# Two more 1 MB places for the experts' weights, and another order in which the chunks use the places

## The reference

```python
def hier_moe(h, router_group_w, router_expert_w, w_gate, w_up, w_down):
    ...   # each token is sent to TOP_K = 2 experts of one group
    def expert_block(args):
        xblk, e = args
        a = xblk @ w_gate[e]          # 1024 x 512
        b = xblk @ w_up[e]            # 1024 x 512
        return (jax.nn.silu(a) * b) @ w_down[e]    # 512 x 1024
    ...   # weighted by the gate and added to the tokens
```

## Time and profile before

| | |
|---|---|
| median of three runs | 1726.66 us (1725.32 to 1726.68) |
| the profiled execution | 1725.77 us |
| its span in the profile | 1724.0 us |
| TensorE busy | 1622.8 us, 94% |
| VectorE busy | 988.2 us, 57% |
| ScalarE busy | 611.1 us, 35% |
| moved by DMA | 415.65 MB, 241 GB/s over the span |

### The profile page before, as it was taken

The page is one execution under the profiler, slowest core; times in us unless marked ns, Lnnn a source line. Parts: engine busy times, 40 slices in busy tenths (PEclk is TensorE's granted clock), DMA queues, the critical chain, the costliest instruction groups (busy, mean ns, idle before and its releaser), DMA issues.

```text
span 1724.0 us, 25871 instructions
## 1 busy us (share of the span) xinstructions
PE 1622.8 (94%) x10376; PEld 1286.3 (75%) x10376; DVE 988.2 (57%) x1660; ACT 611.1 (35%) x809; POOL 57.6 (3%) x82
## 2 busy tenths in 40 slices
PE   7999999999999999999999999999989788878887
PEld 6999857899998999888889998999954344334333
DVE  7788655687867888865478885788331111111112
ACT  5333346434336333465443334653421000000001
POOL 4000005000000000001100000000000000000000
PEclk9999999999999999999999999999989999899999
DMA  7544442545554555544255555332689999999996
GB/s 282 191 182 183 184 183 74 183 184 188 196 232 157 195 197 185 192 155 167 74 191 198 194 185 214 119 145 74 250 371 426 426 428 428 427 428 427 428 427 271
DMA packets 49240, 415.65 MB, mean 241 GB/s; under 512 B 5616, under 2 KB 5648, under 8 KB 7824
## 3 DMA queue, kind: packets, MB, share of 16 engines
q1 hardware_dynamic: 49104, 414.61, 61.1%
q10 hardware_dynamic: 64, 0.03, 0.0%
HBM read 413.54 MB, written 1.05 MB: 240 GB/s over the span
## 4 chain that ended last, share of the span: by engine, by line
PE 73%; DMA 19%; DVE 4%; ACT 3%; issue 1%; SPq 0%; POOL 0%; DVEq 0%; ACTq 0%
PE bank L556 65%; DMA sb_moe_ring<-experts 18%; PE bank L1250 6%; DVE sb_ring_lo L2011 1%; ACT sb_high L1524 1%; DMA sb_ring<-weights 1%; PE bank L745 0%; PE bank L834 0%; DMA sb_h<-xT 0%; SPq L481 0%; DVE sb_x_parts L2040 0%; ACT sb_high_first L1524 0%; DVE sb_nmax L2144 0%; DVE sb_lnv L2047 0%; ACT sb_x_parts L1535 0%
## 5 line engine op out<-in xcount | busy, mean ns | idle before, releaser
L2011 DVE TENSOR_TENSOR sb_ring_lo<-sb_ring,sb_high 128x2304 fp32r<-128x2304 f32 (+4 forms) x180 | 352.1, 1957 | 124.8 <-ACT sb_high L1524 124.3
L556 PE MATMUL bank<-sb_x_parts,sb_high 128*128 128x512 f32 (+1 forms) x1792 | 407.9, 365 | 0.4 <-DVE sb_ring_lo L2011 0.2
L556 PEld LDWEIGHTS bank<-sb_x_parts,sb_high 128*128 128x128 f32 x1792 | 315.1, 187 | 52.5 <-DVE sb_ring_lo L2011 0.9
L1524 ACT ACTIVATE sb_high<-sb_ring 128x3072 fp32r<-128x3072 f32 x100 | 275.2, 2752 | 140.7 <-PE bank L556 112.0
L556 PE MATMUL bank<-sb_x_parts,sb_ring_lo 128*128 128x256 f32 x1632 | 253.0, 279 | 0.0
L556 PEld LDWEIGHTS bank<-sb_x_parts,sb_ring_lo 128*128 128x128 f32 x1632 | 224.3, 189 | 7.4
L556 PE MATMUL bank<-sb_act_hi,sb_ring_lo 128*128 128x256 f32 x704 | 195.4, 278 | 0.0
L556 PE MATMUL bank<-sb_act_hi,sb_high 128*128 128x256 f32 x680 | 189.1, 278 | 2.2 <-DVE sb_ring_lo L2011 1.7
L556 PE MATMUL bank<-sb_act_lo,sb_high 128*128 128x256 f32 x680 | 188.7, 277 | 0.0
L1250 PE MATMUL bank<-sb_moe_ring,sb_act 128*32 128x512 f32 x512 | 131.8, 662 | 40.9 <-DMA sb_moe_ring<-experts 40.7
L1566 ACT ACTIVATE sb_expg<-sb_gate_r 128x256 f32<-128x256 f32 x88 | 36.9, 419 | 338.8 <-DVE sb_gate_r L2074 338.8
(11 more groups left out here) (385 smaller groups left out, 1896.9 us busy)
## 6 DMA issues: line engine op xcount, KB each, us to landing
sb_ring<-weights SPq DMA_DIRECT2D x133, 1536.0 KB, 6.5
sb_moe_ring<-experts SPq DMA_DIRECT2D x185, 1024.0 KB, 20.9
sb_qk<-experts SPq DMA_DIRECT2D x4, 1024.0 KB, 15.0
sb_moe_ring<-experts SPq DMA_DIRECT2D x8, 256.0 KB, 17.8
sb_h<-xT SPq DMA_DIRECT2D x2, 512.0 KB, 6.7
sb_ring<-weights SPq DMA_DIRECT2D x2, 512.0 KB, 7.5
sb_oT<-experts SPq DMA_DIRECT2D x1, 1024.0 KB, 15.4
sb_pin<-pT SPq DMA_DIRECT2D x1, 512.0 KB, 17.7
```

Source lines behind the costliest of these rows:

```text
L556: ins = nc.tensor.matmul(o, l, r, start=start, stop=stop, skip_group_check=True)
L1524: nc.scalar.activation(high_of(n)[:, lo * P:hi * P], ring[:, n % RING, lo * P:hi * P], ACT.Copy).then_inc(done, 1)
L2011: return V.tensor_tensor(ring_lo[:, n % RING, cols], ring[:, n % RING, cols], high_of(n)[:, cols].bitcast(F32), ALU.subtract)
```

## The change

It adds two places. `front` is 15 KB in each partition at the low end of SBUF, made by asking for 1 KB of DMA scratch in place of the usual 16 KB; it holds place 17 (16 tiles) and twelve of the sixteen tiles of place 18. The other four tiles, `last_four`, lie over `act_hi`, a buffer of the feed-forward layers that has moved to stand behind `h`; `x_parts`, `hn` and `sq` therefore lie 2,112 bytes higher. All later buffers and `moe_ring` keep their addresses. Places 17 and 18 are loaded between dense chunks 132 and 133, after the last feed-forward layer (`acc_ready`). Place 18 comes in two transfers.

The order of loading of the other 17 places stays (`MOE_LOADS`). The order in which chunks use them changes: chunks 0 to 11 use the ring's twelve places, chunks 12 and 13 the new ones, chunks 14 to 17 those over `qk`, and chunk 18 that over `oT`. The loads behind the first ones are then chunks 19 to 30, which wait for releases 1 to 12, and the loop of SyncE begins with chunk 31 where it began with 29. Two semaphores that were each used once, `f_ready` and `ba_ready`, become one, `logits_in`.

```diff
-MOE_ONCE = 5
+MOE_ONCE = 7
...
-MOE_ORDER = [6, 7, 8] + _early + [9, 10, 11, 12, 13, 14, 15] + _under_ring[len(_early):] + [16]
+FREE_PLACES = [17, 18]
+_late = _under_ring[len(_early):]
+MOE_LOADS = [6, 7, 8] + _early + [9, 10, 11, 12, 13, 14, 15] + _late + [16]
+MOE_ORDER = [6, 7, 8] + _early + [9, 10, 11] + _late + FREE_PLACES + [12, 13, 14, 15, 16]
...
+        front = sb("front", [P, 30 * P])
...
+        with nc.sbuf_tensor("sb_last_four", [P, 4 * P], F32) as last_four:
+            pass
+        act_hi = inside(sb("act_hi", [P, 2 * T + LINE], F32R), [P, 2, T])
...
-        act_hi = inside(sb("act_hi", [P, 2 * T + LINE], F32R), [P, 2, T])
...
+        def place_parts(place):
+
+            if place == 18:
+                return [(slice(0, 12 * P), front[:, 16 * P:28 * P]), (slice(12 * P, 16 * P), last_four[:, :])]
+            return [(slice(0, MCT * P), moe_place(place)[:, 0:MCT * P])]
...
+            def first_experts(n, place):
+
+                for cols, to in place_parts(place):
+                    sp.dma_start(to, experts[n][:, cols]).then_inc(moe_in[place], 16)
+
             for n in range(whole * RING, N_CHUNKS):
+                if n == N_CHUNKS - 1:
+                    sp.wait_ge(acc_ready, 4 * len(FFNS))
+                    for place in FREE_PLACES:
+                        first_experts(MOE_ORDER.index(place), place)
                 sp.wait_ge(ring_free, n - RING + 1)
                 sp.dma_start(ring[:, n % RING, :], weights[n]).then_inc(slot_in[n % RING], 16)
...
-            for n, place in enumerate(MOE_ORDER):
+            for place in MOE_LOADS:
+                n = MOE_ORDER.index(place)
...
-                sp.dma_start(moe_place(place), experts[n]).then_inc(moe_in[place], 16)
+                first_experts(n, place)
...
-                pe.wait_ge(moe_in[place], r * (16 * QUAD * 6 // MOE_RING) + 16 * uses)
+                pe.wait_ge(moe_in[place], r * (16 * QUAD * 6 // MOE_RING) + 16 * len(place_parts(place)) * uses)
...
-    nc = bacc.Bacc("TRN2", target_bir_lowering=False, num_devices=1)
+    nc = bacc.Bacc("TRN2", target_bir_lowering=False, num_devices=1, dynamic_dma_scratch_size=1024)
```

More of the change, by code:

```diff
@@ L340, in moe_place @@
                 return moe_ring[:, place, :]
-            if place < MOE_FIRST - 1:
+            if place < 16:
                 return moe_once[:, place - MOE_RING, :]
-            return oT[:, :, :].rearrange("p a t -> p (a t)")
+            if place == 16:
+                return oT[:, :, :].rearrange("p a t -> p (a t)")
+            return front[:, (place - 17) * MCT * P:]
+        def place_parts(place):
+            if place == 18:
+                return [(slice(0, 12 * P), front[:, 16 * P:28 * P]), (slice(12 * P, 16 * P), last_four[:, :])]
+            return [(slice(0, MCT * P), moe_place(place)[:, 0:MCT * P])]
         def turned_part(part):
@@ L382, in two_block_kernel @@
         qk_used, qk_padded, dec_rows = sem("qk_used"), sem("qk_padded"), sem("dec_rows")
-        f_ready, logit_abs, logit_ln, logf_ready, dec_sum, dec_ready = (
-            sem("f_ready"), sem("logit_abs"), sem("logit_ln"), sem("logf_ready"), sem("dec_sum"), sem("dec_ready"))
+        logits_in, logit_abs, logit_ln, logf_ready, dec_sum, dec_ready = (
+            sem("logits_in"), sem("logit_abs"), sem("logit_ln"), sem("logf_ready"), sem("dec_sum"), sem("dec_ready"))
         ple_t, ple_e = sem("ple_t"), sem("ple_e")
         silu_in, silu_e = sem("silu_in"), sem("silu_e")
-        ba_ready, bg_ready = sem("ba_ready"), sem("bg_ready")
+        bg_ready = sem("bg_ready")
         rows_ready, gdiff, gdecay, dn_qk, dn_ready = (
@@ L466, in _ @@
                     sp.wait_ge(ring_free, PLAN["mix_out"])
-                elif place < MOE_FIRST - 1:
+                elif place < 16:
                     sp.wait_ge(mix_ready, 2)
@@ L920, in with_gates @@
                 mm(bank[:, :], x[1], w[0], False, last, lin_ready if last else None)
-                mm(gate, x[1], f_hi, False, last, f_ready if last and c else None)
+                mm(gate, x[1], f_hi, False, last, logits_in if last and c else None)
             def two_units(i, ks=range(KD)):
@@ L1037, in _ @@
                     if m < 2:
-                        mm(logits, token_x[1], f_hi, False, last, ba_ready if last and c else None)
+                        mm(logits, token_x[1], f_hi, False, last, logits_in if last and c else None)
                     tl.used()
@@ L1267, in arrived @@
                 place, uses = place_of(i)
-                pe.wait_ge(moe_in[place], r * (16 * QUAD * 6 // MOE_RING) + 16 * uses)
+                pe.wait_ge(moe_in[place], r * (16 * QUAD * 6 // MOE_RING) + 16 * len(place_parts(place)) * uses)
             def four_tiles(at, t, width=4):
                 place, _ = place_of(at + t // MCT)
+                if place == 18 and t % MCT >= 12:
+                    return last_four[:, (t % MCT - 12) * P:(t % MCT - 12 + width) * P]
                 return moe_place(place)[:, (t % MCT) * P:(t % MCT + width) * P]
@@ L2404, in _ @@
             fox_heads(0)
-            dve.wait_ge(f_ready, 1)
+            dve.wait_ge(logits_in, 1)
             zf = small[:, 32:64]
@@ L2490, in ba_logits @@
             def ba_logits():
-                dve.wait_ge(ba_ready, 1)
+                dve.wait_ge(logits_in, 2)
                 ba = B[3][:, 0:16].rearrange("p (c n) -> p c n", n=8)
```

## The result

The changed kernel takes 1730.57 us (median of nine runs, 1729.82 to 1732.52) against 1726.66 us before. Over all runs compared, the ratio is 1.003 with a 95% interval of 1.0021 to 1.0038: it is slower by 3.6 to 6.6 us. One of the nine runs of the kernel before took 2028.45 us and is not in the ratio. The profiled span grew from 1724.0 to 1728.1 us. The forecast was 1724.3 us and a range of 1721.4 to 1727.0, so it missed, and on the wrong side.

A forecast was written before the change was run, and what follows sets the result against it. TensorE was taken to bound the kernel until near 1240 us, transfers after; 4.9 us less for two chunks, 1.9 to 3.4 more for a second hole, taken as -2.4: 1726.66 - 2.4 = 1724.3 us, range 1721.4 to 1727.0.

The forecast's parts named there:

- Buffers moved: Feed-forward operands shifted by 2,112 bytes, `act_hi` further: no work added, matmuls of 277 and 276 ns alike, so 0.
- Rival 3: TensorE's first 1240 us: operands' new place lengthens `x_parts` matmuls, 3 ns each, 10.3 us, giving 1734.6 us; chance 0.08.
- Two chunks early, hidden: Early loads between dense chunks 132 and 133, in a stretch 80% idle: cost nothing, gain at most 4.9 us.
- The hole stays: Gap in the transfers from 1272 to 1275 us keeps its length; first release still at 1274.0 us.
- Chunk 31: First load of SyncE's loop, after release 20: can land at 1309.6 us, all 4.9 us kept.
- Chunk 32: Load after release 21, issued at 1309.2 us to dry engines: 3.0 to 2.5 us kept, perhaps 1.5.
- The Trainium skill's knee: Restart at chunk 32: lone 1 MB estimated at 4.4 us, landing at 1313.6 us, 3.4 us kept; rows preferred.
- The order of the places alone: Loads behind the hole wait for releases 1 to 12 rather than up to 16: gives nothing.

The follow-up runs named there:

- p2: Kernel before with small DMA scratch, `lnv` at the low end of SBUF, `act_hi` 64 bytes higher and `x_parts` unmoved: 1732.61 us, single run.
- e2: Kernel before with only the smaller scratch, unused `front` and the changed kernel's addresses of the moved buffers: 1732.63 us, ratio 1.0038.
- e1: Changed kernel with `act_hi`, `x_parts`, `hn` and `sq` back at their old addresses: 1723.38 us against 1725.86 for the kernel before, ratio 0.9988.
- e3: e1 with only one of the two new places, place 17: 1725.89 us against 1726.29 for the kernel before, ratio 0.9997.
- e5: e1 with the two new places loaded a second time, by chunks 30 and 31: 1720.75 us, ratio 0.9971 to the kernel before.
- e4: e1 with the places used in the order of before, the new ones ahead of the last: 1723.42 us, single run.
- p3: Kernel before with small DMA scratch, `lnv` at the low end of SBUF, `x_parts` and `act_hi` both 128 bytes higher: 1731.27 us, single run.
- p7: Kernel before with small DMA scratch, `lnv` at the low end of SBUF, `x_parts` 2112 and `act_hi` 2304 bytes higher: 1729.80 us, single run.

## Why the prediction was wrong

*Buffers moved: "I take 0".* This is the step that failed, and the whole of the miss. I weighed the moved operands by the offset within 128 bytes, compared `act_hi` (277 ns) with `act_lo` (276), and found them equal at two offsets. The runs fit a period of 256 bytes, and show, by p2, that an operand's duration also hangs on the one its matmuls alternate with. Two equal rows of one layout said nothing about another layout. Measured: 6.1 us by the busy time of the five groups, 5.6 us by the loads of the four feed-forward layers, and e2 6.8 us by the medians.

*Rival 3.* It named the mechanism, the place and the point from which it decides (0.7 ns a matmul). It was priced at 3 ns on 3424 matmuls, 10.3 us, which gave 1734.6 us. The mean of `x_parts` on `ring_lo` rose by 4 ns and that on `high` (366 for 365) hardly, 4.7 us in all; `act_hi` and `act_lo` rose by 1.4 us, which the price left out. Its chance of 0.08 was too small, since nothing in the trace could price an operand at another address, and the range should have reached it.

*Two chunks early, hidden: nothing.* Right. The window carries 168 GB/s, and e1's dense part is on time (chunk 133 at 1212.7 us).

*The hole stays.* Right; 3 us at 1278.5 us, and the share there is 0.00.

*Chunk 31: "All 4.9 us are kept here".* Not quite: 4.5 us by the landings. It landed 5.4 us after an issue at 1311.1 us, and a first dip opened ahead of it (0.46 for 1.5 us). I took the landing of chunk 30 as the moment at which the engines run dry; the dip began 1.8 us before it. The error is under half a microsecond at this landing, and it is the one that broke the expectation of e3, where it took the whole 2.45 us.

*Chunk 32: kept 3.0 to 2.5, then perhaps 1.5; "what is kept at chunk 32 is kept in the last landing".* Right in cause, and the sum of 2.4 us came out, but its terms did not, so its closeness is in part luck. Issue to landing took 4.8 us as said; release 21 came 0.4 us sooner after the first load than before (34.8 against 35.2 us), so 3.3 us were kept at this landing. Chunk 33, issued 4.2 us ahead of the landing of chunk 32, landed 3.2 us after it, and the 2.6 us that were left ended as 2.4. The prediction had one dip of 1 to 2 us; there are two, worth 2.5 us together. e5 confirms the cause: with the wait for release 21 taken off the stream, the whole 4.9 us of two places are kept.

*The Trainium skill's knee.* (SBUF — State Buffer, section "The DMA setup-cost knee".) By its fit a lone megabyte takes an estimated 4.4 us. Every such landing here took longer: 4.8 us at 1280.5 us, and 4.8 and 5.3 us before. The one at 1315.3 us, into a queue that had all but run dry, took 4.8 us. So the rows were the better price of a restart. The 3.3 us kept at chunk 32 lie near that rule's 3.4 because release 21 came sooner, and not because the landing was shorter.

*The order of the places alone: nothing.* Right, by e4.

## What to carry to other kernels

A buffer that moves is an edit to every instruction that reads it. Where one engine bounds a stage with thousands of matmuls, compare the mean ns of each group, old and new, and keep each operand's start within 256 bytes as it was when something is put ahead of it; up to 4 ns a matmul cost more here than two megabytes loaded early could win. More places in front of a full transfer stream help only as far as the releases behind them come in time, and a place used once delays all later ones: loading it a second time was worth as much as adding it.

## What the runs showed of the hardware

The start of TensorE's fp32r operands within 256 bytes changed the matmul's duration: from 278 to 280 and 283 ns for 128x256 from `x_parts` (p3, p7), and from 276 to 282 for `act_lo`, which had not moved, when `act_hi` started at the same offset as it. 256 and 512 bytes more changed nothing. Which pairs of starts are good, and what in the memory or the engine makes it so, stays open: four starts of `act_hi` and three of `x_parts` are too few for a rule, the fourth layer of p7 shows other durations at the same starts, and the address of the stationary tiles was not varied.

A load issued 2.2 to 2.4 us ahead of the previous landing landed 2.9 to 5.2 us after it in four traces, and not 2.45. The margin of a stream must be counted from the moment at which the rate falls, which lay 1.8 us ahead of the landing in the changed kernel. In the kernel before 5.2 to 5.6 us ahead of the previous landing were enough (chunks 29, 30 and 32 landed 2.6, 2.3 and 2.45 us after it); how much is just enough was not measured. Between the dips and the end the transfers held 427 GB/s (share 1.01).
